# Attention of a hybrid layer rebuilt as one run of 64 steps, with values as weights and scores as three fp32r products

## The reference

```python
for i in range(L // Q_BLOCK):
    q0 = i * Q_BLOCK
    kv_len = q0 + Q_BLOCK
    s = jnp.einsum('bhqd,bhkd->bhqk', q[:, :, q0:kv_len], k[:, :, :kv_len]).astype(jnp.float32) * scale
    mask = chunk_id[None, :kv_len] <= chunk_id[q0:kv_len, None]
    s = jnp.where(mask, s, neg)
    p = jax.nn.softmax(s, axis=-1).astype(v.dtype)
    outs.append(jnp.einsum('bhqk,bhkd->bqhd', p, v[:, :, :kv_len]))
```

## Time and profile before

| | us |
|---|---|
| median of 3 runs | 1295.06 |
| the runs | 1305.39, 1293.5, 1295.06 |
| the profiled execution | 1303.91 |
| its span | 1302.2 |
| PE busy in it | 1172.9 |
| DVE busy | 972.1 |
| ACT busy | 716.5 |
| POOL busy | 356.3 |

### The profile page before, as it was taken

The page is one execution under the profiler, slowest core; times in us unless marked ns, Lnnn a source line. Parts: engine busy times, 40 slices in busy tenths (PEclk is TensorE's granted clock), DMA queues, the critical chain, the costliest instruction groups (busy, mean ns, idle before and its releaser), DMA issues.

```text
span 1302.2 us, 16421 instructions
## 1 busy us (share of the span) xinstructions
PE 1172.9 (90%) x5604; PEld 919.9 (71%) x5604; DVE 972.1 (75%) x1152; ACT 716.5 (55%) x859; POOL 356.3 (27%) x341
## 2 busy tenths in 40 slices
PE   5899989958898899999399999999999999999992
PEld 3447465646777777787378888888888887787771
DVE  1969998173555575337589999999989998898871
ACT  5511216364444464122357777777777777777750
POOL 2313014126255200011103233333323333443220
PEclk9899988688999999999589999999999999999996
DMA  6600010003000201223669999999999999999940
GB/s 202 151 1 1 1 18 9 1 1 130 1 0 0 97 1 33 82 97 122 243 279 387 366 387 387 387 401 389 384 376 372 382 365 366 371 354 367 360 134 10
DMA packets 55475, 260.80 MB, mean 200 GB/s; under 512 B 31088, under 2 KB 31760, under 8 KB 41616
## 3 DMA queue, kind: packets, MB, share of 16 engines
q1 hardware_dynamic: 45344, 243.03, 48.6%
q0 software_dynamic: 10096, 17.34, 5.5%
HBM read 252.25 MB, written 26.35 MB: 214 GB/s over the span
## 4 chain that ended last, share of the span: by engine, by line
PE 63%; DVE 15%; DMA 12%; ACT 3%; issue 3%; SPq 2%; POOL 0%; DVEq 0%; ACTq 0%; POOLq 0%
PE psum L2052 24%; DMA w<-in_w 10%; PE psum L2072 9%; PE psum L1967 6%; DVE arena L1301 5%; PE psum L1893 5%; PE psum L1927 4%; DVE arena L1103 3%; PE psum L1913 3%; PE psum L1745 2%; DMA out<-arena 2%; PE psum L2042 1%; PE psum L1850 1%; PE psum L1879 1%; PE psum L2058 1%
## 5 line engine op out<-in xcount | busy, mean ns | idle before, releaser
L1635 DVE TENSOR_TENSOR w_rest<-w,w_high 128x2048 fp32r<-128x2048 f32 x136 | 305.2, 2286 | 21.5 <-ACT w_high L1025 21.5
L1025 ACT ACTIVATE w_high<-w 128x2048 fp32r<-128x2048 f32 x136 | 256.4, 1913 | 87.8 <-DMA w<-in_w 52.2
L2052 PE MATMUL psum<-w_high,xgT_high 128*128 128x512 f32 x544 | 218.5, 402 | 14.0 <-DVE xgT_rest L1628 14.0
L2052 PE MATMUL psum<-w_rest,xgT_high 128*128 128x512 f32 x544 | 214.5, 394 | 0.0
L2052 PE MATMUL psum<-w_high,xgT_rest 128*128 128x512 f32 x544 | 214.1, 394 | 0.0
L1642 DVE TENSOR_TENSOR w_rest<-w,w_high 128x2048 fp32r<-128x2048 f32 x68 | 152.5, 2285 | 1.8 <-ACT w_high L1035 1.8
L1035 ACT ACTIVATE w_high<-w 128x2048 fp32r<-128x2048 f32 x68 | 126.4, 1908 | 20.8 <-DMA w<-in_w 20.6
L2052 PEld LDWEIGHTS psum<-w_high,xgT_high 128*128 128x128 f32 x544 | 103.5, 190 | 39.4 <-issue 14.8
L660 POOL DMA_INDIRECT out<-arena,idx x34 | 91.6, 2695 | 109.2 <-DVE arena L1655 106.1
L2052 PEld LDWEIGHTS psum<-w_rest,xgT_high 128*128 128x128 f32 x544 | 103.4, 190 | 22.1
L2052 PEld LDWEIGHTS psum<-w_high,xgT_rest 128*128 128x128 f32 x544 | 103.7, 191 | 20.5
(11 more groups left out here) (266 smaller groups left out, 2105.6 us busy)
## 6 DMA issues: line engine op xcount, KB each, us to landing
w<-in_w SPq DMA_DIRECT2D x102, 2048.0 KB, 18.5
arena<-in_x SPq DMA_DIRECT2D x5, 1024.0 KB, 6.2
h_scratch<-arena SPq DMA_DIRECT2D x8, 512.0 KB, 2.6
out<-arena SPq DMA_DIRECT2D x8, 512.0 KB, 3.6
arena<-in_x SPq DMA_DIRECT2D x1, 3072.0 KB, 10.0
arena<-in_w_in SPq DMA_DIRECT2D x1, 2688.0 KB, 16.2
arena<-in_w_in SPq DMA_DIRECT2D x1, 2048.0 KB, 12.2
wout_y_raw<-in_w_out SPq DMA_DIRECT2D x1, 2048.0 KB, 7.9
```

The costliest lines, as they stand in the source:

```text
L1025: act.activation(w13h[k][:, c, :], w13[b][k][:, c, :], ACT.Copy).then_inc(W13H_READY[k], 1)
L1635: dve.tensor_tensor(w13l[b][k][:, c, :], w13[b][k][:, c, :], w13h[k][:, c, :].bitcast(F32), S_).then_inc(W13_SPLIT[k], 1)
L2052: last = pe.matmul(psum[:, k, :], x_[:, c, :], w_[:, c, :], start=(c == 0 and n == 0), stop=(c == KC - 1 and n == 2))
```

## The change

The four passes become one run of 64 steps, unrolled. The order within a head is now 7, 6, 1, 0, 5, 4, 3, 2, so that steps come in pairs of neighbouring tiles.

- Scores: q and k are kept as a high part in fp32r and the rest in fp32r. `scores(n)` is three products, each at least 256 columns wide.
- Turning of q and k: in four quarters (`turn_head`), through bank 7, at steps 1 to 4 of the head before. Of each quarter ACT writes the high part (`high_part`) and then DVE the rest (`rest_part`), which needs the high part. PE turns the next quarter when the rest of the one before is saved.
- Values: 64 columns of v are the weights and the 128 columns of a turned block move. The two tiles of a pair write partitions 0 to 63 and 64 to 127 of bank 6, block by block in turn. The result is transposed: DVE copies it (`save_ohT`), PE turns it back (`turn_values`), DVE scales both tiles (`save_o`).
- SP loads `wOr` when the last scores are filled, not at `mid_done`; its place in memory holds the rest parts of q and k. ACT waits for it at the first piece of it.
- The last `turn_values` and the wait for `o_saved` stand after the first `project_out`.

```diff
-        qT = [at(S0 + 1024 * b, T) for b in range(2)]
-        kT = [at(S0 + 2048 + 1024 * b, T) for b in range(2)]
+        qTh = [own(f"qT_high_{b}", S0 + 1024 * b, 1, T, F32R)[:, 0, :] for b in range(2)]
+        kTh = [own(f"kT_high_{b}", S0 + 2048 + 1024 * b, 1, T, F32R)[:, 0, :] for b in range(2)]
+        qTl = [own(f"qT_rest_{b}", 35904 + 1024 * b, 1, T, F32R)[:, 0, :] for b in range(2)]
+        kTl = [own(f"kT_rest_{b}", 35904 + 2048 + 1024 * b, 1, T, F32R)[:, 0, :] for b in range(2)]
...
-            sp.dma_start(wOr, w_out_c[:, 0:OC, :]).then_inc(wout_in, 16)
             sp.wait_ge(heads_made, H)
             sp.dma_start(x2[:, 0:NT - 2, :], x_s[:, 0:NT - 2, :]).then_inc(x_again, 16)
+            sp.wait_ge(s_filled, STEPS)
+            sp.dma_start(wOr, w_out_c[:, 0:OC, :]).then_inc(wout_in, 16)
...
-        STEPS = 2 * NT
-        tile_of = [(NT - 1 - n % NT // 2) if n % 2 == 0 else n % NT // 2 for n in range(STEPS)]
+        STEPS = H * NT
+        ORDER = [i for k in range(NT // 4) for i in (NT - 1 - 2 * k, NT - 2 - 2 * k, 2 * k + 1, 2 * k)]
+        tile_of = [ORDER[n % NT] for n in range(STEPS)]
+        PAIRS = STEPS // 2
         fills_of = [i // 4 + 1 for i in tile_of]
         first_fill = [sum(fills_of[:n]) for n in range(STEPS + 1)]
         FILLS = first_fill[STEPS]
+        pair_of = [n // 2 for n in range(STEPS) for _ in range(fills_of[n])]
...
+        Y_PIECE_AT = {STEPS - 2 * NT + n: k for k, n in enumerate((1, 2, 4, 6, 8, 10, 11, 12))}
+        HEAD_BANK = 7
+        def next_part(n):
+            return (n // NT + 1, n % NT - 1) if n // NT + 1 < H and 1 <= n % NT <= 4 else None
...
+            def high_part(h, part):
+                k = part // 2
+                high, bank = ((kTh, 4 + k), (qTh, 6 + k))[part % 2]
+                act.wait_ge(head_turned, 4 * h + part + 1)
+                act.activation(high[h % 2][0:QH, 512 * k:512 * (k + 1)], psum[0:QH, HEAD_BANK if h else bank, :],
+                               ACT.Copy).then_inc(head_high, 1)
...
+                if n + 2 < STEPS:
+                    exponentials(n + 2)
+                if next_part(n):
+                    high_part(*next_part(n))
+                if n in Y_PIECE_AT:
+                    high_y_piece(Y_PIECE_AT[n])
...
+            def rest_part(h, part):
+                k = part // 2
+                high, rest, bank = ((kTh, kTl, 4 + k), (qTh, qTl, 6 + k))[part % 2]
+                dve.wait_ge(head_high, 4 * h + part + 1)
+                dve.tensor_tensor(rest[h % 2][0:QH, 512 * k:512 * (k + 1)], psum[0:QH, HEAD_BANK if h else bank, :],
+                                  high[h % 2][0:QH, 512 * k:512 * (k + 1)].bitcast(F32), S_).then_inc(head_saved, 1)
...
+            def save_ohT(m):
+                dve.wait_ge(pv_done, m + 1)
+                dve.tensor_copy(ohT[m % 2], psum[:, 6, 0:P]).then_inc(ohT_saved, 1)
+            def save_o(m):
+                for n in (2 * m, 2 * m + 1):
                     a = am[:, n % 4, :]
-                    dve.wait_ge(p_ready, it16 + (n + 1))
+                    dve.wait_ge(p_ready, n + 1)
                     dve.reciprocal(a[:, 2:3], a[:, 1:2]).then_inc(sum_inv, 1)
-                    dve.wait_ge(sum_inv, it16 + (n + 1))
-                    dve.wait_ge(pv_done, itF + first_fill[n + 1])
-                    dve.tensor_scalar(otok[:, tile_of[n], bass.ds((2 * it + n // NT) * VD, VD)],
-                                      psum[:, 6 + n % 2, 0:VD], a[:, 2:3], None, M_).then_inc(o_saved, 1)
...
+                if n % 2 == 0 and n >= 2:
+                    save_o(n // 2 - 1)
+                if n + 2 < STEPS:
+                    row_max(n + 2)
+                if next_part(n):
+                    rest_part(*next_part(n))
+                if n % 2 == 1:
+                    save_ohT(n // 2)
+                if n - 1 in Y_PIECE_AT:
+                    rest_y_piece(Y_PIECE_AT[n - 1])
...
-                            last = pe.matmul(psum[:, 6 + n % 2, 0:VD], probT[f % 4][:, j - j0, :],
-                                             vtok[:, j, bass.ds((2 * it + n // NT) * VD, VD)], start=(j == 0), stop=(j == i))
...
+            def turn_head(h, part):
+                k, a = part // 2, 1 - part % 2
+                buf = (qn, kn)[a][h % 2]
+                if part == 0:
+                    pe.wait_ge(heads_made, h + 1)
+                if h >= 1:
+                    pe.wait_ge(head_saved, 4 * h + part)
+                bank = HEAD_BANK if h else 6 - 2 * a + k
+                for i in range(4 * k, 4 * k + 4):
+                    last = pe.transpose(psum[0:QH, bank, (i % 4) * P:(i % 4 + 1) * P], buf[:, i, :], ident[:, :])
+                last.then_inc(head_turned, 1)
...
+                for m, (q_, k_) in enumerate(((qTh, kTh), (qTl, kTh), (qTh, kTl))):
                     for k in range((L + 511) // 512):
-                        w = min(512, L - 512 * k)
-                        last = pe.matmul(psum[:, 2 * (n % 2) + k, 0:w], qT[b][0:QH, i * P:(i + 1) * P], kT[b][0:QH, 512 * k:512 * k + w],
-                                         start=True, stop=True)
-                    last.then_inc(s_filled, 1)
...
+                        w = max(2 * P, min(512, L - 512 * k))
+                        last = pe.matmul(psum[:, 2 * (n % 2) + k, 0:w], q_[h % 2][0:QH, i * P:(i + 1) * P],
+                                         k_[h % 2][0:QH, 512 * k:512 * k + w], start=(m == 0), stop=(m == 2))
+                last.then_inc(s_filled, 1)
...
+            def values(m):
+                if m >= 1:
+                    pe.wait_ge(o_saved, 2 * m)
+                h, tiles = 2 * m // NT, tile_of[2 * m:2 * m + 2]
+                saved(first_fill[2 * m + 2] - 1)
+                for j in range(tiles[0] + 1):
+                    for k in range(2):
+                        if j <= tiles[k]:
+                            last = pe.matmul(psum[k * VD:(k + 1) * VD, 6, 0:P], vtok[:, j, h * VD:(h + 1) * VD],
+                                             probT[(first_fill[2 * m + k] + j // 4) % 4][:, j % 4, :],
+                                             start=(j == 0), stop=(j == tiles[k]))
+                last.then_inc(pv_done, 1)
+            def turn_values(m):
+                pe.wait_ge(ohT_saved, m + 1)
+                pe.transpose(psum[:, 6, P:2 * P], ohT[m % 2], ident[:, :]).then_inc(otok_filled, 1)
...
+            for n in range(STEPS):
+                turn_probs(n)
+                if n % 2 == 0 and n >= 2:
+                    turn_values(n // 2 - 1)
+                if n + 2 < STEPS:
+                    scores(n + 2)
+                if next_part(n):
+                    turn_head(*next_part(n))
+                if n % 2 == 1:
+                    values(n // 2)
...
+                    turn_values(PAIRS - 1)
+                    pe.wait_ge(o_saved, H * NT)
```

224 lines of the change are left out of this document (87 added, 137 removed).

## The result

The change makes the kernel slower. Over the runs that can be compared, its time is 1.0232 times that of before, with a 95% interval of 1.0176 to 1.0288: some 30 us on 1295. (Four executions gave 1333.57, 1328.81, 1326.62 and 3994.83 us; the last is left out, and the median of the others is 1328.81.) In the later runs the kernel before had 11 to 19 executions each time, with medians of 1299 to 1304 us; against those the loss is 25 to 30 us. The profiled execution took 1333.57 us with a span of 1331.8, where before's took 1303.91. So 29.7 us have to be found between the two traces.

What follows compares the result with a forecast made beforehand. PE bound the kernel before; afterwards DVE and ACT in series bind attention. 8.5 + 7 x 25.3 + 17.0 + 5.5 = 208.1, +1, less 199.7: +9.4; clock +5; 1295 + 14 = 1309.5 us (profiled 1318), range 1275 to 1345, forecast's own 1290 to 1328.

Steps and rivals of the forecast that it cites:

- The walk of a head: Attention head with turning, DVE and ACT in series: 25.3 us, with PE waits of 2.0, 1.7 and 2.3 us.
- PE's work, 17.9 us a head: PE's own work per attention head falls from 21.2 to 17.1 us, plus 0.8 for changes to halves and back.
- The clock, +5 us: PE's pauses in attention lower its clock: some 3 us a fall, two of three heads, half hidden; +5 us.
- The pieces, 5.5 us: Eight projection pieces on DVE, 1.2 to 1.3 us each; five of them move the path, adding 5.5 us.
- The last head, 17.0 us: The last attention head turns nothing for a next one; the same walk gives 17.0 us.
- The start, 8.5 us: Attention's start, from 16 transposes to the first exponential: 8.5 us, where before it was 9.8.
- The load of the attention's out weights is hidden: Second half's load, 12.6 us from the last scores on, hidden by about 5 us; uncovered, at most 12.6.
- The last turning back, 1 us: Turning back the last values after the first projection lets PE wait 1 us.
- The experts' part shifts as a whole: The experts' matmuls and weight loads behind the attention are untouched and only move in time; no term.
- PE as the bound: Rival: ACT's and DVE's series in attention is shorter than walked, PE stays the bound; 1250 to 1285 us, chance 0.18.
- Halves that don't overlap: Rival: array halves don't overlap in the values, 0.107 an instruction, 3.8 us a head, +30: 1340 us; chance 0.07.
- The lower clock throughout: Rival: PE's lower clock holds through the attention, +80 us, or +25 for a third of the time; 1330 to 1385, chance 0.15.

Runs made afterwards that it cites:

- e1: The change with ACT's high part of the next head's quarter moved ahead of the exponential of n+2; 1293.94 us, 0.9929 of before.
- e2: The change plus unread transposes on PE filling the first and third of its pauses, order otherwise kept; 1317.32 us, 1.0109 of before.
- e4: The change with the eight projection pieces spread over the heads from the second on, not steps 49 to 60; 1321.57 us, 1.0162 of before.
- e10: As e9, but with the projection pieces placed where e9's trace has engines waiting for PE; 1273.30 us, 0.9789 of before.
- e11: As e8 with the three products, but the projection pieces moved: ACT's as in e10, DVE's to other steps; 1285.42 us, 0.9863 of before.
- e8: The change with e1's order and e4's places for the projection pieces; 1296.06 us, 0.9948 of before.
- e9: As e8, but scores are one fp32 product and DVE has no rest part; 1284.20 us, 0.9874 of before.

## Why the prediction was right or wrong

The side was right, and the mechanism. The size was not: +14.4 us against some +30. The result lies in the wide range and at the upper edge of the forecast's own, 1290 to 1328: 1325 us by the ratio (1.023 x 1295), 1328.81 by the median.

- **The walk of a head** (25.3 us, with waits of 2.0, 1.7 and 2.3). Right: the head at full clock takes 25.57, with 1.86, 1.46 and 2.16, each released by the row named. e1 shows that the cause is the one walked: the high part behind the exponential.
- **PE's work, 17.9 us a head.** Too low: PE is busy 19.3 us in the head of 25.57. Some of this is the way busy time is counted, since half of the last pass before has 21.9 us for a sum of 21.2. The forecast did not rest on it, since the pauses absorb most of it. Of its terms, the values were right (30 in 1.96 us with its tail, 0.06 each, the halves overlap) and the fp32r products of 256 columns too (0.12 each, as at 363.09: 0.28 less a tail of some 0.16). So was the 0.1 us for going to halves at full clock: a quarter of four transposes takes 0.53 us when values follow (310.65 to 311.18) and 0.44 when other full-width work does (341.90 to 342.34).
- **The clock, +5 us.** The step that failed: the kind of loss was right, the term too small. First, its own factors (seven heads, a fall in two of three, 3 us with half of it hidden) multiply to 7.0 and not to 5. The first six whole heads lost 7.0: 1.55 us in each of the first four (27.13 against 25.57, and e2), nothing in the fifth, 0.74 in the sixth. That the two 7.0 agree is partly luck, since what a fall costs depends on its place: behind the last of the three pauses nothing hid it, behind the first the other two did in part. Second, the term had nothing for the start. It ran at 0.53, and the first values came after 15.2 us against 11.9 walked, 3.3 more; e4, with the same instructions there and a clock of 0.74, has 13.5.
- **The pieces, 5.5 us.** From the values at 471.61 to the projection at 520.12 are 48.5 us; one head at full clock and e4's last one without a piece (25.57 + 13.96) are 39.5. So pieces and clock together cost 9.0 us there, 3.5 more than the term. How they share it stays open: no run had pieces there and a full clock with the change's order. e2 has 0.93 in this stretch instead of 0.84 and takes 48.8 us, no less, which speaks for the pieces; but the transposes that it adds may be in the way.
- **The last head, 17.0 us**, of which 13.6 from its first values on. Right: e4 has 13.96 without pieces.
- **The start, 8.5 us.** 10.1 (296.02 to 306.13): too short, at a clock of 0.53.
- **The load of the attention's out weights is hidden.** Right: issued at 511.57, and landed after 7.8 us, where it took 12.6 before. **The last turning back, 1 us**: 1.8 with the lower clock beside it.
- **The experts' part shifts as a whole.** In the profiled pair it is 4.2 us longer, in no part that the change touches. This share was in no term.
- **The rivals.** PE as the bound: no, but one exchange on ACT (e1) makes it nearly so, at 21.57 us a head. The limit given for it is off: by the terms that make 22 us a head 1286 us (8.5, 17.0, 5.5, 1 and 5 beside the heads), 1% faster begins at 21.4 us a head and not at 21.8, and e1's 21.57 came with 0.7%. Halves that don't overlap: no. The lower clock throughout: no, the attention has 0.89 on the whole; but a lower clock than in the sum is 5.3 us of the miss (2.0 in the heads, 3.3 in the start) and an open share of the 3.5 behind them.

In numbers, the sum made the attention 213.1 us long (208.1, and 5 for the clock) and it is 224.1, 11.0 more: 3.3 in the start, 2.0 for the clock in the heads, 3.5 for pieces and clock in the last 48.5 us, and 2.2 that the walk was short (0.27 in each of seven heads, 0.4 in the last). These are 11.0 of the 15.3 us by which the profiled execution missed 1318.3; 4.2 are the experts' part, 0.8 the projection's start, less 0.7 for the earlier start.

## What to carry to other kernels

Before putting new work into two engines that already take turns, write down the order of each: an instruction whose operand is ready must not stand behind one that waits for the other engine, and here the exchange of two neighbouring rows was worth 33 us. Pieces of other work were free here inside a wait that the trace shows and that is longer than the piece (e10); a piece a little longer than its wait cost a head 0.3 us (e11), and one outside such waits 1.6 to 1.9 us (e8, e9). And a pause on PE costs more than its length where the clock falls behind it; filling it (e2) gives back just that share, removing it (e1) gives back both.
